# Down weights gated in every feed-forward round, sums that begin with x1, and closings on one engine

## Chip, cores and metric

The kernel runs on one core of one Trainium2 chip. The metric is the device time of one execution in microseconds (us). Before the change the median of three runs is 1894.62 us, the lowest 1893.93 and the highest 1896.67. Lower is better.

## What is computed

One encoder layer in float32 over two sequences, a prompt of 256 tokens and a sample of 1024, with a model width of 1024. A conditioning vector for each sequence gives six modulation vectors, among them the gate `g2` of the feed-forward part, so prompt and sample have different gates. The first half of the layer is attention with 16 heads and an output projection. Its result is `x` after the first layer norm, called x1 below. The second half is a gated feed-forward net of width 2816:

```python
x = _layer_norm(alpha * x + g1 * mix, ln1_g, ln1_b)          # x1

u2 = _layer_norm(x) * (1 + sc2) + sh2
f = (jax.nn.silu(u2 @ w_gate) * (u2 @ w_up)) @ w_down
return _layer_norm(alpha * x + g2 * f, ln2_g, ln2_b)          # alpha = 2 ** 0.25
```

`g2` scales the columns of `f`, which are the columns of `w_down`: `g2 * (h @ w_down)` is `h @ (w_down * g2)`.

## The kernel before

The program has five stages: modulation, projections, attention, output and the feed-forward part, which is the function `channel`. All tokens, 256 of the prompt and then 1024 of the sample, lie in ten tiles of 128. Every matrix product is made in three passes, since a float32 operand is split into a rounded high half (a copy on ScalarE) and a low half (a subtraction on VectorE): high by high, low by high and high by low (lines 218, 219 and 220). Engines run their own programs and meet by semaphores. The order of the work is written out by hand.

**Attention.** Softmax is taken with a row of negated maxima that is added to the scores through one extra row of the query tile. VectorE writes that row (line 1365), and SyncE issues a DMA that puts it in its place (line 1092) once for each of the 16 heads, g = 0 to 15. TensorE makes the scores (lines 1162 and 1163) after it has landed (`m_in`), ScalarE the exponentials (line 1295). In front of the first row SyncE's queue has the projections' stores to HBM (lines 461 and 462), and ScalarE has nothing between its last projection work and the first exponential.

**Feed-forward.** The hidden width is taken in 22 rounds f of 128 columns, and the tokens in three chunks c: tokens 0 to 256 (the prompt, tiles 0 and 1), 256 to 768 (tiles 2 to 5) and 768 to 1280 (tiles 6 to 9). A round's work:

- SyncE loads the gate and up weights of the round into `raw_gu` and the down weights into `raw_d` (lines 1832 and 1834). A load waits for the low half of the round before, the last reader of the buffer.
- ScalarE makes the high halves of `raw_gu` (line 1955) and of `raw_d` (line 1961), VectorE the low halves (lines 2058 and 2062). Each of the four has two slots, and rounds alternate between them.
- TensorE makes, for each chunk, first the down products of the *round before* for the chunk's tiles, each into one of two PSUM buffers, and then gate and up of *this* round. A down tile waits until the tile two before it was added (`dn_added`).
- ScalarE makes the silu of a chunk (line 1970) and the high half of the hidden values (line 1975), VectorE their product (line 2070) and low half (line 2076). VectorE adds each down tile to the running sum `sum_f` in SBUF (line 2122); round 0's tiles begin it with a copy (line 2119).

In a round VectorE's list for a chunk is: first add, product of the chunk before, second add, hidden low half, other adds. Behind chunk 1 stands the down weights' low half, behind chunk 2 the low half of the next round's gate and up weights.

GpSimd loads `g2`, one broadcast row for each sequence, into `gate_2` (line 1857) when the output stage is complete, and has nothing else to do until the end.

**The end.** The last round but one is added for chunks 1, 2, 0, and TensorE's list is: its down tiles of chunk 1, last gate and up of chunk 1, down tiles of chunk 2, gate and up of chunk 2, down tiles of chunk 0, then the last round's down tiles of chunk 1, gate and up of chunk 0, and the last down tiles of chunks 2 and 0. The sum of the rounds before the last is multiplied by `g2` on GpSimd (line 1862), x1 is read back from HBM (line 1844), and VectorE merges `alpha * x1` with it (line 2083). The last round alone has gated down weights (lines 2163 and 2167, the sample's in the additional buffer `down_raw_gated`). Then each tile has a last add with its row sum (line 2090), a mean and squares on ScalarE (lines 2003 and 2005), a centring with the gain on VectorE (line 2100), a root on ScalarE and a reciprocal on VectorE (line 2105). VectorE closes four of the ten tiles, 5, 8, 0 and 1, with one instruction (line 2112); the other six are scaled by ScalarE (line 2015) and closed by an add on GpSimd (line 1866). SyncE stores each tile (line 1850).

## Time and profile before

| | us |
|---|---|
| median of three runs | 1894.62 |
| the profiled execution, its own time | 1893.81 |
| span of that execution in the trace | 1892.0 |
| TensorE busy (93%) | 1754.2 |
| VectorE busy (61%) | 1146.1 |
| ScalarE busy (38%) | 710.0 |
| GpSimd busy (12%) | 224.8 |

The span goes from the first to the last instruction in the trace; the execution's own time is 1.8 us longer. Busy time is an average over stages that differ: it doesn't say which engine ends last in a stage. In the rows below, PE is TensorE, PEld its weight loads, DVE VectorE, ACT ScalarE, POOL GpSimd, and a q behind an engine's name is its queue of DMA issues. PEclk is the clock granted to TensorE as a share of full speed. In a timeline the bracket names what ended the idle time before the instruction, and how long that was.

### The profile page before, as it was taken

The page shows a single profiled execution, that of the slowest core. Times are in us where ns is not written, and L with a number is a line of the kernel's source. Part 1 is how long each engine was busy: PE and PEld are TensorE (multiplying, and loading weights), DVE is VectorE, ACT ScalarE, POOL GpSimd, SP SyncE. Part 2 cuts the span into 40 slices and gives each one's busy share as a digit, 9 for nine tenths or more (in the row PEclk, how much of TensorE's full clock was granted, in tenths as well). Part 3 has the DMA queues.
Part 4 walks back from the last instruction along what each step waited for, and adds up shares of the span by engine and source line. Part 5 has one row for each costly group of instructions (what it writes and reads, how often), then busy time and mean ns, then how long its engine had stood idle before and what let it go on. Part 6 is the DMA issues. An engine that isn't in the chain of part 4 may idle for free. (4 is left out here: it accounts for less than half of the span.)

```text
span 1892.0 us, 22484 instructions
## 1 busy us (share of the span) xinstructions
PE 1754.2 (93%) x8562; PEld 1385.6 (73%) x8562; DVE 1146.1 (61%) x1380; ACT 710.0 (38%) x1102; POOL 224.8 (12%) x237
## 2 busy tenths in 40 slices
PE   5898955999999999898999999999999999999993
PEld 3898943656667777677788888878888888878872
DVE  3888875878778776588644443444343443344388
ACT  3566543767667667654411111111111111111114
POOL 1123443101222210000000000000000000000063
PEclk8999976999999999999999999999999999999997
DMA  9133457545635541432411111111111111111123
GB/s 358 50 119 113 130 164 187 172 125 182 149 84 139 122 107 45 160 106 82 141 34 34 34 44 33 33 33 44 45 33 33 33 36 42 33 33 34 55 89 134
DMA packets 128534, 171.54 MB, mean 91 GB/s; under 512 B 15160, under 2 KB 100920, under 8 KB 125392
## 3 DMA queue, kind: packets, MB, share of 16 engines
q1 hardware_dynamic: 113184, 105.64, 18.0%
q0 software_dynamic: 12528, 46.61, 9.2%
q10 hardware_dynamic: 2752, 18.37, 3.0%
q8 instruction: 42, 0.69, 0.1%
q14 instruction: 28, 0.23, 0.0%
HBM read 128.21 MB, written 42.30 MB: 90 GB/s over the span
## 5 line engine op out<-in xcount | busy, mean ns | idle before, releaser
L2122 DVE TENSOR_TENSOR sum_f<-pair,sum_f 128x1024 f32<-128x1024 f32 x200 | 244.0, 1220 | 474.6 <-PE pair L220 473.1
L218 PE MATMUL pair<-u_hi,w_out_hi 128*128 128x512 f32 (+1 forms) x1056 | 377.2, 357 | 0.0
L220 PE MATMUL pair<-u_hi,w_out_hi 128*128 128x512 f32 (+1 forms) x1056 | 377.0, 357 | 0.0
L219 PE MATMUL pair<-u_lo,w_out_hi 128*128 128x512 f32 (+1 forms) x1056 | 376.6, 357 | 0.0
L1970 ACT ACTIVATE silu_gate<-pair 128x512 f32<-128x512 f32 (+1 forms) x63 | 33.1, 526 | 577.1 <-PE pair L220 577.1
L219 PEld LDWEIGHTS pair<-u_lo,w_out_hi 128*128 128x128 f32 x1056 | 198.6, 188 | 33.0
L218 PEld LDWEIGHTS pair<-u_hi,w_out_hi 128*128 128x128 f32 x1056 | 198.6, 188 | 32.9 <-DVE w_out_hi L1717 0.2
L220 PEld LDWEIGHTS pair<-u_hi,w_out_hi 128*128 128x128 f32 x1056 | 198.4, 188 | 32.5
L1349 DVE TENSOR_TENSOR p_lo<-p_f,p_hi 128x1024 fp32r<-128x1024 f32 (+1 forms) x144 | 167.2, 1162 | 42.8 <-ACT p_hi L1299 42.4
L218 PE MATMUL pair<-down_hi,hidden_hi 128*128 128x512 f32 x440 | 182.4, 415 | 9.7 <-DVEq L2093 6.1
L1295 ACT ACTIVATE p_f<-pair 128x1024 f32<-128x1024 f32 (+1 forms) x144 | 140.6, 976 | 132.9 <-PE pair L1163 61.9
L1357 DVE TENSOR_REDUCE max_col<-pair 128x1 f32<-128x1024 f32 x128 | 155.7, 1221 | 51.4 <-PE pair L1219 51.3
L219 PE MATMUL pair<-down_lo,hidden_hi 128*128 128x512 f32 x440 | 172.9, 393 | 0.0
L220 PE MATMUL pair<-down_hi,hidden_lo 128*128 128x512 f32 x440 | 172.6, 392 | 0.0
L1299 ACT ACTIVATE p_hi<-p_f 128x1024 fp32r<-128x1024 f32 (+1 forms) x144 | 145.8, 1012 | 4.6
L1862 POOL TENSOR_TENSOR sum_f<-sum_f,gate 128x1024 f32<-128x1024 f32 x10 | 29.9, 3010 | 880.9 <-DVE sum_f L2122 880.9
L218 PEld LDWEIGHTS pair<-down_hi,hidden_hi 128*128 128x128 f32 x440 | 82.9, 188 | 57.4 <-DVE sum_f L2122 33.4
L218 PE MATMUL pair<-p_hi,v_hi 128*65 128x512 f32 (+1 forms) x288 | 111.9, 389 | 2.0 <-DVE p_lo L1349 1.3
L219 PE MATMUL pair<-p_lo,v_hi 128*65 128x512 f32 (+1 forms) x288 | 109.9, 382 | 0.0
L220 PE MATMUL pair<-p_hi,v_lo 128*65 128x512 f32 (+1 forms) x288 | 109.8, 381 | 0.0
L1219 PE MATMUL pair<-k_a,q_a 128*128 128x512 f32 (+3 forms) x288 | 95.0, 415 | 13.2 <-DVE max_col L1357 6.5
L1975 ACT ACTIVATE hidden_hi<-hidden_f 128x512 fp32r<-128x512 f32 (+1 forms) x63 | 35.4, 561 | 168.1 <-DVE hidden_f L2070 168.1
(258 smaller groups left out, 2928.0 us busy)
## 6 DMA issues: line engine op xcount, KB each, us to landing
w_ada_late<-in_w_ada ACTq DMA_DIRECT2D x16, 1024.0 KB, 5.1
gate_up_raw<-in_w_gate SPq DMA_DIRECT2D x21, 512.0 KB, 4.0
gate_up_raw<-in_w_up SPq DMA_DIRECT2D x21, 512.0 KB, 5.2
down_raw<-in_w_down SPq DMA_DIRECT2D x21, 512.0 KB, 3.2
w_ada_first<-in_w_ada SPq DMA_DIRECT2D x8, 1024.0 KB, 13.9
o_tile<-o SPq DMA_DIRECT2D x10, 512.0 KB, 4.0
x<-y SPq DMA_DIRECT2D x10, 512.0 KB, 2.6
gate_up_raw<-x SPq DMA_DIRECT2D x10, 512.0 KB, 3.6
```

The costliest lines, as they stand in the source:

```text
L218: pe.matmul(out, a[0], b[0], start=start, stop=False)
L219: pe.matmul(out, a[0], b[1], start=False, stop=False)
L220: return pe.matmul(out, a[1], b[0], start=False, stop=stop)
L1219: mm = pe.matmul(dst, qs[0][s][0:w, q], ks[0][n][0:w, key], start=True, stop=True)
L1295: act.activation(pf[:, c % PS, 0:w], src, ACT.Exp, scale=scale).then_inc(e_done, 1)
L1299: act.activation(ph[0][:, c % PS, 0:w], pf[:, c % PS, 0:w], ACT.Copy).then_inc(p_hi, 1)
L1349: dve.tensor_tensor(ph[1][:, c % PS, 0:w], pf[:, c % PS, 0:w], ph[0][:, c % PS, 0:w], ALU.subtract).then_inc(p_lo, 1)
L1357: dve.reduce_max(mcol[:, NTP + i:NTP + i + 1], a_pair(m)[:, :, :].rearrange("p a b -> p (a b)"), AX.X).then_inc(a_free, 1)
L1862: pool.tensor_tensor(sumf[:, t, :], sumf[:, t, :], g2[:, int(t >= NTP), :], ALU.mult).then_inc(gated, 1)
L1970: act.activation(sg[:, 0:hi - lo], k.bank[(slot + c + 1) % 2][:, 0, 0:hi - lo], ACT.Silu).then_inc(silu_done, 1)
L1975: act.activation(hid[0][:, lo:hi], hf[:, 0:hi - lo], ACT.Copy).then_inc(hid_hi, 1)
L2122: dve.tensor_tensor(sumf[:, t, :], src, sumf[:, t, :], ALU.add).then_inc(dn_added, 1)
```

## The change

1. **Row 0 of the maxima** is issued by ScalarE, ahead of its first exponential. SyncE issues rows 1 to 15 as before.
2. **The gate lies in the down weights of every round.** The two slots of the down halves become two pairs of single buffers: `down_hi`, `down_lo` for the sample and `down_prompt_hi`, `down_prompt_lo` for the prompt. In each round SyncE loads the same down weights twice into `raw_d`. VectorE multiplies the first copy by the prompt's gate, the second by the sample's, and high and low halves are made of each. Per round that is one load, one copy on ScalarE and three instructions on VectorE more than before. Round 0's first product waits for `g2`.
3. **The sums begin with x1.** SyncE loads ten tiles of x1 into `sum_f` when the output stage is complete, ahead of the second down load of round 0, and the first addition is `alpha * x1 + product` in one instruction. At the end the reads of x1, the merges, GpSimd's multiplications and the buffer `down_raw_gated` fall away.
4. **VectorE closes all ten tiles.** ScalarE's scalings and GpSimd's adds fall away; GpSimd has no work left in the feed-forward part but the loads of `g2`.
5. **The last rounds.** TensorE makes the last but one round's down tiles of chunk 0 first instead of after the second gate-up chunk, so that this round is added in the order of the tiles.

The diff, without the lines that only take names away or lines that repeat:

```diff
-                k.wd = [k.sb(weights, f"down_{s}", [P, 2, D], F32R) for s in ("hi", "lo")]
+                k.wd = [k.sb(weights, f"down_{s}", [P, D], F32R) for s in ("hi", "lo")]
+                k.wdp = [k.sb(weights, f"down_prompt_{s}", [P, D], F32R) for s in ("hi", "lo")]
...
 
-        for g in range(H):
+        for g in range(1, H):
...
         k.all_read(act)
+        act.wait_ge(m_row, 1)
+        act.dma_start(qs[1][0][DA:DA + 1, :].bitcast(F32), mrow[:, :].bitcast(F32)).then_inc(m_in, 16)
...
@@ -1826,27 +1824,30 @@
...
         wg, wu, w_dn = rows(k.i["w_gate"][0]), rows(k.i["w_up"][0]), rows(k.i["w_down"][0])
 
-        def load(f):
+        def load_gate_up(f):
             sp.wait_ge(gu_lo, f)
             for m, w in enumerate((k.i["w_gate"][0], k.i["w_up"][0])):
                 sp.dma_start(raw_gu[:, m, :, :], rows(w)[:, :, bass.ds(f * P, P)]).then_inc(gu_in, 16)
-            sp.wait_ge(d_lo, f)
+
+        def load_down(f, part):
+            sp.wait_ge(d_lo, 2 * f + part)
             sp.dma_start(raw_d[:, :], k.i["w_down"][0][bass.ds(f * P, P), :]).then_inc(d_in, 16)
 
         sp.wait_ge(k.mix_ready, NT)
-        load(1)
-        with sp.Fori(2, NF) as f:
-            load(f)
-        sp.wait_ge(gu_lo, NF)
-        for i, t in enumerate(LAST_TILES):
-            if i >= 2:
-                sp.wait_ge(merged, i - 1)
-            sp.dma_start(x1[i % 2], k.x1[t * P:(t + 1) * P, :]).then_inc(x1_in[i % 2], 16)
+        load_gate_up(1)
+        after_output(sp)
+        for t in range(NT):
+            sp.dma_start(sumf[:, t, :], k.x1[t * P:(t + 1) * P, :]).then_inc(x1_in, 16)
+        load_down(0, 1)
+        load_down(1, 0)
+        with sp.Fori(2, NF - 1, 2) as f:
+            for m in range(2):
+                load_gate_up(f + m)
+                load_down(f + m - 1, 1)
+                load_down(f + m, 0)
+        load_down(LF, 1)
         for t in LAST_TILES:
-            if t in ON_DVE:
-                sp.wait_ge(dve_out, sorted(ON_DVE, key=PLACE.get).index(t) + 1)
-            else:
-                sp.wait_ge(out_ready, ON_POOL.index(t) + 1)
+            sp.wait_ge(dve_out, PLACE[t] + 1)
...
         after_output(pool)
         for s in range(2):
             pool.dma_start(g2[:, s, :], k.mod[s, 5 * D:6 * D].partition_broadcast(P)).then_inc(g2_in, 16)
-        pool.wait_ge(g2_in, 32)
-        for i, t in enumerate(LAST_TILES):
...
-            pool.wait_ge(dn_added, NT * (LF - 1) + i + 1)
-            pool.tensor_tensor(sumf[:, t, :], sumf[:, t, :], g2[:, int(t >= NTP), :], ALU.mult).then_inc(gated, 1)
...
@@ -1872,9 +1863,11 @@
             place = t if place is None else place
...
+            hi, lo = wdp if t < NTP else wd
             for m in range(2):
+                cols = slice(m * 512, (m + 1) * 512)
                 mm = three(pe, k.bank[2 + t % 2][:, m, :], [x[:, t * P:(t + 1) * P] for x in hid],
-                           [w[:, 1 - slot, m * 512:(m + 1) * 512] for w in wd], True, True)
+                           [hi[:, cols], lo[:, cols]], True, True)
...
                     pe.wait_ge(hid_lo, NCH * (f - 1) + c + 1)
                     if c == 0:
-                        pe.wait_ge(d_lo, f)
+                        pe.wait_ge(d_lo, 2 * f - 1)
+                    if c == 1:
+                        pe.wait_ge(d_lo, 2 * f)
                     for t in TILES[c]:
...
         def before_last_down(c):
 
...
-            pe.wait_ge(d_lo, LF)
+            pe.wait_ge(d_lo, 2 * LF - (c == 0))
             for t in TILES[c]:
-                down(LF, t, 1, PLACE[t])
+                down(LF, t, 1)
 
...
+            pe.wait_ge(d_lo, 2 * NF - (c == 0))
             for t in TILES[c]:
-                down(NF, t, 1 if c == 0 else 0, PLACE[t])
+                down(NF, t, 0, PLACE[t])
 
         def finale():
+            before_last_down(0)
             before_last_down(1)
             last_gate_up(0)
             before_last_down(2)
             last_gate_up(1)
-            before_last_down(0)
             last_down(0)
...
-        def d_round(f, slot, first):
-            act.wait_ge(d_in, 16 * (f + 1))
+        def prompt_round(f, first):
+            act.wait_ge(d_gated, 2 * f + 1)
             if not first:
-                act.wait_ge(dn_ready, NT * (f - 1))
-            act.activation(wd[0][:, slot, :], raw_d[:, :], ACT.Copy).then_inc(d_hi, 1)
+                act.wait_ge(dn_ready, NT * (f - 1) + NTP)
+            act.activation(wdp[0][:, :], raw_d[:, :], ACT.Copy).then_inc(d_hi, 1)
+
+        def sample_round(f, first):
+            act.wait_ge(d_gated, 2 * f + 2)
+            if not first:
+                act.wait_ge(dn_ready, NT * f)
+            act.activation(wd[0][:, :], raw_d[:, :], ACT.Copy).then_inc(d_hi, 1)
...
                 if not (first and c == 0):
                     silu(f, c, slot)
                 if c == 1:
-                    d_round(f, slot, isinstance(f, int) and f < 2)
+                    prompt_round(f, isinstance(f, int) and f == 0)
                 if c == 2:
                     gu_round(f + 1, 1 - slot, isinstance(f, int) and f == 0)
+                    sample_round(f, isinstance(f, int) and f == 0)
...
         def finale():
             silu(LF, 0, 1)
-            act.wait_ge(wd_gated, 1)
-            act.wait_ge(dn_ready, NT * (LF - 1))
-            act.activation(wd[0][:, 1, :], raw_s[:, :], ACT.Copy).then_inc(d_hi, 1)
+            prompt_round(LF, False)
             last_silu(0)
+            sample_round(LF, False)
             last_silu(1)
             for m, g in enumerate(("ln2_g", "ln2_b")):
...
             dve.wait_ge(gu_hi, f + 1)
             dve.tensor_tensor(wgu[1][:, slot, :, :, :], raw_gu[:, :, :, :], wgu[0][:, slot, :, :, :], ALU.subtract).then_inc(gu_lo, 1)
 
-        def d_low(f, slot):
-            dve.wait_ge(d_hi, f + 1)
-            dve.tensor_tensor(wd[1][:, slot, :], raw_d[:, :], wd[0][:, slot, :], ALU.subtract).then_inc(d_lo, 1)
+        def gate_prompt(f):
+            dve.wait_ge(d_in, 32 * f + 16)
+            dve.tensor_tensor(raw_d[:, :], raw_d[:, :], g2[:, 0, :], ALU.mult).then_inc(d_gated, 1)
...
+        def prompt_low(f):
+            dve.wait_ge(d_hi, 2 * f + 1)
+            dve.tensor_tensor(wdp[1][:, :], raw_d[:, :], wdp[0][:, :], ALU.subtract).then_inc(d_lo, 1)
...
 
             i = PLACE[t]
             dve.wait_ge(dn_ready, NT * LF + i + 1)
-            dve.wait_ge(merged, i + 1)
+            dve.wait_ge(dn_added, NT * (LF - 1) + t + 1)
             dve.scalar_tensor_tensor(z[:, t, :], k.bank[2 + t % 2][:, :, :].rearrange("p a b -> p (a b)"), 1.0, sumf[:, t, :],
...
             if isinstance(f, int) and f == 1:
-                dve.tensor_copy(sumf[:, t, :], src).then_inc(dn_added, 1)
+                if t == 0:
+                    dve.wait_ge(x1_in, 16 * NT)
+                dve.scalar_tensor_tensor(sumf[:, t, :], sumf[:, t, :], ALPHA, src, ALU.mult, ALU.add).then_inc(dn_added, 1)
...
                         hidden_low(f, c)
+                if c == 0 and not first:
+                    gate_prompt(f)
                 if c == 1:
-                    d_low(f, slot)
+                    if first:
+                        dve.wait_ge(g2_in, 32)
+                        gate_prompt(f)
+                    prompt_low(f)
                 if c == 2:
+                    gate_sample(f)
                     gu_low(f + 1, 1 - slot)
+                    sample_low(f)
...
         def finale():
-            add(LF, 2, 0)
+            add(LF, 0)
             product(LF, 0, 1)
-            add(LF, 3, 1)
+            add(LF, 1)
             hidden_low(LF, 0)
-            dve.wait_ge(g2_in, 32)
-            dve.wait_ge(d_in, 16 * NF)
-            dve.tensor_tensor(raw_s[:, :], raw_d[:, :], g2[:, 1, :], ALU.mult).then_inc(wd_gated, 1)
-            add(LF, 4, 2)
-            add(LF, 5, 3)
-            dve.wait_ge(wd_gated, 1)
-            dve.tensor_tensor(raw_d[:, :], raw_d[:, :], g2[:, 0, :], ALU.mult).then_inc(wd_gated, 1)
-            dve.wait_ge(d_hi, NF)
-            dve.tensor_tensor(wd[1][:, 1, :], raw_s[:, :], wd[0][:, 1, :], ALU.subtract).then_inc(d_lo, 1)
-            merge(2)
-            merge(3)
+            gate_prompt(LF)
+            for t in TILES[1]:
+                add(LF, t)
+            prompt_low(LF)
             last_product(0)
-            add(LF, 6, 4)
             last_low(0)
-            add(LF, 7, 5)
-            merge(4)
-            add(LF, 8, 6)
...
+            for t in TILES[2]:
+                add(LF, t)
+            sample_low(LF)
             last_product(1)
-            add(LF, 0, 8)
             last_low(1)
-            add(LF, 1, 9)
-            dve.wait_ge(d_hi, NF + 1)
-            dve.tensor_tensor(wd[1][:, 0, :], raw_d[:, :], wd[0][:, 0, :], ALU.subtract).then_inc(d_lo, 1)
             for t in (2, 3, 4, 5):
                 last_add(t)
```

VectorE's order where round 0 passes into round 1, before the change (`pair` is a PSUM buffer, `w_out_hi` the memory of the gate-up halves, the shapes are those of the output):

```order
L2070 TENSOR_TENSOR hidden_f32<-pair0,silu_gate 128x256
L2076 TENSOR_TENSOR hidden_lo<-hidden_f32,hidden_hi 128x256
L2062 TENSOR_TENSOR down_lo<-down_raw,down_hi 128x1024
L2070 TENSOR_TENSOR hidden_f32<-pair1,silu_gate 128x512
L2076 TENSOR_TENSOR hidden_lo<-hidden_f32,hidden_hi 128x512
L2058 TENSOR_TENSOR w_out_hi<-gate_up_raw,w_out_hi 128x2x8x128
L2119 COPY sum_f<-pair2 128x1024
```

and after it:

```order
L2069 TENSOR_TENSOR hidden_f32<-pair0,silu_gate 128x256
L2075 TENSOR_TENSOR hidden_lo<-hidden_f32,hidden_hi 128x256
L2049 TENSOR_TENSOR down_raw<-down_raw,gate_2 128x1024
L2057 TENSOR_TENSOR down_prompt_lo<-down_raw,down_prompt_hi 128x1024
L2069 TENSOR_TENSOR hidden_f32<-pair1,silu_gate 128x512
L2075 TENSOR_TENSOR hidden_lo<-hidden_f32,hidden_hi 128x512
L2053 TENSOR_TENSOR down_raw<-down_raw,gate_2 128x1024
L2045 TENSOR_TENSOR w_out_hi<-gate_up_raw,w_out_hi 128x2x8x128
L2061 TENSOR_TENSOR down_lo<-down_raw,down_hi 128x1024
L2113 SCALAR_TENSOR_TENSOR sum_f<-sum_f,pair2 128x1024
```

Two products with `gate_2` stand there now, the second in front of the low half of round 1's gate and up weights, and the sum's first instruction is a multiply-add on itself instead of a copy.

SyncE's issues at the start of the feed-forward part, before (the branch opens the loop of the rounds):

```order
L1825 UNCONDITIONAL_BRANCH
L1832 DMA gate_up_raw<-in_w_gate 128x8x128
L1832 DMA gate_up_raw<-in_w_up 128x8x128
L1834 DMA down_raw<-in_w_down 128x1024
L1838 UNCONDITIONAL_BRANCH
L1832 ISA
L1832 DMA gate_up_raw<-in_w_gate 128x8x128
```

and after:

```order
L1823 UNCONDITIONAL_BRANCH
L1830 DMA gate_up_raw<-in_w_gate 128x8x128
L1830 DMA gate_up_raw<-in_w_up 128x8x128
L1840 DMA sum_f<-x1 128x1024 x10
L1834 DMA down_raw<-in_w_down 128x1024 x2
L1843 UNCONDITIONAL_BRANCH
L1830 ISA
```

Ten loads of x1 stand between the gate-up weights of round 1 and the down loads, of which there are two in a row: round 0's second and round 1's first.

VectorE's last rows before (L2100 centres, L2105 inverts, L2112 closes):

```order
L2105 RECIPROCAL std_e<-std_e 128x1
L2100 SCALAR_TENSOR_TENSOR sum_f<-final_rows,neg_mean 128x1024
L2105 RECIPROCAL std_e<-std_e 128x1
L2100 SCALAR_TENSOR_TENSOR sum_f<-final_rows,neg_mean 128x1024
L2105 RECIPROCAL std_e<-std_e 128x1
L2112 SCALAR_TENSOR_TENSOR final_rows<-sum_f,std_e,final_rows 128x1024
L2100 SCALAR_TENSOR_TENSOR sum_f<-final_rows,neg_mean 128x1024 x2
L2105 RECIPROCAL std_e<-std_e 128x2
L2112 SCALAR_TENSOR_TENSOR final_rows<-sum_f,std_e,final_rows 128x1024 x2
```

and after, where the same are L2092, L2097 and L2104:

```order
L2104 SCALAR_TENSOR_TENSOR final_rows<-sum_f,std_e,final_rows 128x1024
L2097 RECIPROCAL std_e<-std_e 128x1
L2092 SCALAR_TENSOR_TENSOR sum_f<-final_rows,neg_mean 128x1024
L2104 SCALAR_TENSOR_TENSOR final_rows<-sum_f,std_e,final_rows 128x1024
L2097 RECIPROCAL std_e<-std_e 128x1
L2092 SCALAR_TENSOR_TENSOR sum_f<-final_rows,neg_mean 128x1024
L2104 SCALAR_TENSOR_TENSOR final_rows<-sum_f,std_e,final_rows 128x1024
L2092 SCALAR_TENSOR_TENSOR sum_f<-final_rows,neg_mean 128x1024
L2097 RECIPROCAL std_e<-std_e 128x2
L2104 SCALAR_TENSOR_TENSOR final_rows<-sum_f,std_e,final_rows 128x1024 x2
```

A closing now stands between nearly every two centrings.

## Rows read from the trace of the kernel before

**Rows 1.** Stretches by engine: from, length, busy us and instructions each, PEclk, DMA, GB/s.

```profile
944.00:1799.00 855.00, 852.79 (x4083) 691.36 (x4082) 364.79 (x360) 120.37 (x160) 0.00 (x0) 1.00 0.13 37
1799.00:1892.00 93.00, 59.39 (x264) 46.02 (x262) 82.67 (x72) 29.80 (x53) 47.03 (x16) 0.85 0.32 113
```

**Rows 2.** Timeline before the first scores: start, length, engine, line; releaser in brackets.

```profile
304.01 0.28 DVE L1365 TENSOR_SCALAR neg_max_row<-pair 10x128 fp32r<-10x128 f32 x1 [0.47 <-PE pair L1225]
...
307.40 1.65 SPq L461 DMA_DIRECT2D kn_t_lo_rows<-x_hat  x1
309.10 0.89 SPq L1092 DMA_DIRECT2D q_b<-neg_max_row  x1
312.28 1.16 POOL L1120 MEMSET k_b<- 1x1280 f32 x1 [19.81 <-DMA kn_t_lo_rows<-x_hat]
...
312.33 0.55 PE L1162 MATMUL pair<-q_a,k_a 128*128 128x256 f32 x1 [6.71 <-issue]
...
313.63 1.28 ACT L1295 ACT_TABLE_LOAD   x1 [24.35 <-PE pair L1163]
```

**Rows 3.** DMA issues of the whole span: KB each, median us to landing.

```profile
down_raw<-in_w_down SPq DMA_DIRECT2D x21, 512.0 KB, 3.2
...
gate<-mod_rows POOLq DMA_DIRECT2D x2, 512.0 KB, 4.3
...
va_hi_rows<-va_hi SPq DMA_DIRECT2D x10, 64.0 KB, 1.5
...
v_hi<-va_hi_rows POOLq DMA_DIRECT2D x2, 320.0 KB, 11.9
```

**Rows 4.** Stretches by engine: the first loads.

```profile
5.00:10.00 5.00, 0.00 (x0) 0.00 (x0) 2.98 (x6) 1.58 (x3) 0.00 (x0) 1.00 1.03 419
```

**Rows 5.** Timeline of round 0 and the first down tiles.

```profile
931.66 1.11 POOL L1857 DMA_DIRECT2D gate<-mod_rows  x2 [157.90 <-DVE u_lo L1725]
...
932.70 1.04 ACT L1961 ACTIVATE down_hi<-down_raw 128x1024 fp32r<-128x1024 f32 x1
...
933.77 1.23 DVE L2062 TENSOR_TENSOR down_lo<-down_raw,down_hi 128x1024 fp32r<-128x1024 f32 x1 [0.52 <-ACT down_hi L1961]
...
938.11 2.29 DVE L2058 TENSOR_TENSOR w_out_hi<-gate_up_raw,w_out_hi 128x2048 fp32r<-128x2048 f32 x1 [1.12 <-ACT w_out_hi L1955]
...
944.25 0.40 PE L218 MATMUL pair<-down_hi,hidden_hi 128*128 128x512 f32 x1
...
947.01 0.28 PE L218 MATMUL pair<-u_hi,w_out_hi 128*128 128x256 f32 x1
```

**Rows 6.** Stretches by engine: around TensorE's pause at the end of the output stage.

```profile
921.40:924.90 3.50, 0.37 (x2) 0.00 (x0) 3.40 (x6) 0.29 (x1) 0.00 (x0) 1.00 0.37 150
924.90:930.00 5.10, 5.03 (x19) 4.14 (x20) 0.01 (x1) 3.87 (x9) 0.00 (x0) 0.67 0.76 206
```

**Rows 7.** Groups of instructions: VectorE's adds, 944 to 1799.

```profile
L2122 DVE TENSOR_TENSOR sum_f<-pair,sum_f 128x1024 f32<-128x1024 f32 x190 | 231.9, 1221 | 465.3 <-PE pair L220 463.9
```

**Rows 8.** Timeline of the end: TensorE's first matmuls, VectorE's closing run.

```profile
1798.81 0.40 PE L218 MATMUL pair<-down_hi,hidden_hi 128*128 128x512 f32 x1
...
1804.90 0.39 PE L218 MATMUL pair<-u_hi,w_out_hi 128*128 128x512 f32 x1
...
1816.09 0.39 PE L218 MATMUL pair<-down_hi,hidden_hi 128*128 128x512 f32 x1
...
1851.67 0.42 DVE L2148 TENSOR_TENSOR hidden_f<-pair,silu_gate 128x256 f32<-128x256 f32 x1 [2.31 <-ACT silu_gate L1994]
...
1852.01 1.27 DVE L2100 SCALAR_TENSOR_TENSOR sum_f<-final_rows,neg_mean 128x1024 f32<-128x1024 f32 x1
...
1886.35 2.48 DVE L2112 SCALAR_TENSOR_TENSOR final_rows<-sum_f,std_e,final_rows 128x1024 f32<-128x1024 f32 x2
```

**Rows 9.** Groups of instructions: VectorE, 1799 to 1892.

```profile
L2112 DVE SCALAR_TENSOR_TENSOR final_rows<-sum_f,std_e,final_rows 128x1024 f32<-128x1024 f32 x4 | 9.0, 2276 | 0.1
...
L2105 DVE RECIPROCAL std_e<-std_e 128x1 f32<-128x1 f32 x4 | 0.6, 150 | 0.0
```

67 lines of the change are left out of this document (22 added, 45 removed).

## Prediction

> **What bounds the kernel now.** I read the stretches first. In the feed-forward rounds TensorE is busy 852.8 of 855.0 us at full clock, VectorE only 364.8 [rows 1]. There the bound is TensorE, and other engines' work is free as long as no wait reaches it. The last 93 us differ: TensorE 59.4, VectorE 82.7, GpSimd 47.0 [rows 1], and the program ends with VectorE's last two closing instructions [rows 8]. Then I looked for the holes in TensorE's row next to the three places that the change touches. Before the first attention scores it stands for 6.71 us, released by nothing the profile names, 3 us after SyncE issues row 0 [rows 2]. At the start of round 1 it has no hole: round 1's gate-up begins at 947.01 [rows 5], and its weights' low half, begun at 938.11 and 2.29 long, was ready at 940.4. That slack of 6.6 us is what the change spends.
>
> **Row 0.** VectorE has the row at 304.29, but SyncE's queue still has stores to issue, the last of them at 307.40, and issues the row at 309.10; TensorE starts at 312.33 [rows 2]. ScalarE has idled 24.35 us by then [rows 2] and now issues it at about 304.35. How long it travels the trace doesn't show for this queue: 1.5 us is the median of SyncE's 64 KB stores [rows 3], 3.2 us what the row took on SyncE's queue behind stores (309.10 to 312.33). So it lands between 305.8 and 307.6. I take 307.0, nearer the upper end since the engines are full of stores: TensorE starts 5.3 us earlier (4.7 to 6.5). What follows is TensorE, ScalarE and VectorE waiting on each other, with no time fixed from outside before the feed-forward, so the gain is kept.
>
> The Trainium skill (DMA: Bandwidth & Descriptors, section Issuing engines are not separate DMA queues) speaks against such a move: all issuing engines share the same 16 DMA engines, and another issuer saves only the time to start a transfer. By that rule the saving would be 309.10 less 304.35, 4.8 us, as that time is large here.
>
> **Round 0.** Three transfers now gate it. (a) Ten rows of x1 go out on SyncE's queue once u2 is complete, at about 931.4; the two gate rows go out on GpSimd's at 931.66 [rows 5]. That is 12 times 0.52 MB, 6.3 MB; long bursts moved at 419 GB/s [rows 4], so 15.0 us. (b) VectorE's prompt product waits for the gate rows. They took 4.3 us alone [rows 3]; sharing the engines evenly with x1 they need about 2.1 MB of traffic, 5 us, from 933: 938.2. Then the product, the high copy and the low half, 1.23 (priced as the low half of the same two-operand form), 1.04 and 1.23 [rows 5], give 941.9. The first down tiles, at 944.25 [rows 5], don't notice. (c) Only then is the second down load issued, behind x1 on the same queue: 931.4, 1 us to start, 15.0, its own 1.25, and half a microsecond to land, 949.2. VectorE sits on it with the low half of round 1's gate-up weights queued behind: product and low half, 1.2 and 2.3, end at 952.8. TensorE needs that at 947.0, so it stops for **5.8 us**. ScalarE's copy of the gate-up high half is in front of its own wait and is not late.
>
> After a hole of 3.5 us the next 5.1 us ran at a mean clock of 0.67 [rows 6], which is 3.4 us at half speed, 1.7 us lost. For a hole of 5.8 I put 2.1. Round 0 costs **7.9 us**. The low bound is a load that needs only its usual 3.2 us [rows 3] from 941.9: 945.1, TensorE at 948.7, cost 1.7. The high bound is the first rival.
>
> **Rounds 1 to 20.** Each gets two products and one more low half on VectorE (3 times 1.22, from the 1.23 of rows 5), one more copy on ScalarE (1.04) and one more load. VectorE idles 465.3 us before the adds [rows 7], 23.3 per round, so 3.7 fit. Position counts more than the sum. The prompt product stands behind the second add of a round, while TensorE runs the 256-column chunk of about 5.6 us. The sample product, the gate-up low half and the sample low half follow the last add, 4.7 us within a chunk of 11.2 us [rows 8]. The order of adds, hidden products and hidden low halves, which sets the short stalls of today, is unchanged. The loads have over 8 us each from issue to use, against 3.2 [rows 3]. So nothing. Without that cover it would be up to 3.7 us times 20. The first adds become multiply-adds of the same operand sizes: nothing.
>
> **The end.** Counted from round 20's first down tile, 1798.81, the span ends 93.2 us later [rows 8]. A tile costs 1.38 (947.01 less 944.25, halved, [rows 5]), a 512-column chunk 11.2 (1804.90 to 1816.09 [rows 8]). Now ten tiles and two chunks precede the last ones: 13.8 and 22.4. Stalls: the fifth tile waits for the third's add, behind two adds, product, hidden low half and gate product: 1.9 in all. After the first chunk the third tile waits for an add behind silu, product, copy, low half and gate product: 5.2 against two tiles' 2.75, so 2.5. Sum 40.6. Then four tiles (5.5), one stall of 1.5 for the first closing add, the 256-column chunk (5.6) and silu: the last hidden product starts at 53.7, where before it was 52.9 (1851.67).
>
> From there VectorE runs without a gap: product and low half 0.42 each, ten centrings at 1.27, six last adds at 1.3 (an add of 1.22 [rows 7] and its accumulator), ten closings at 1.24 (half of the last 2.48), seven small reciprocals at 0.15 [rows 9], less 0.08 of overlap at each of some 35 starts (the first product ends 0.08 after the next start at 1852.01 [rows 8]): 33.0 us. Before, the same run took 37.2 (1851.67 to 1888.83 [rows 8]), with four closings of mean 2276 ns beside GpSimd [rows 9]; GpSimd is silent now, so 1.24 stands. With the 3.2 us of the last store: 53.7, 33.0 and 3.2 make 89.9, a gain of 3.3; I take **3.0**, as a hole of 2.5 us can cost some clock. Bounds: 0 (two such losses of 1.7) and 5.0 (no stalls of the first kind).
>
> **The sum.** 5.3 and 3.0 off, 7.9 on: minus 0.4 against the profiled execution's 1893.81 (span 1892.0, 1.8 around it), 1893.4. The median of the three runs lies 0.8 above that execution, so I put the time at 1894.0, no measurable difference. Bound by bound (row 0 4.7 to 6.5; round 0 from 5.8 without clock loss to 10.7 with a tenth less bandwidth and twice the loss; end 0 to 5) the independent errors give about 4 us either way.
>
> **Rivals.**
> 1. *Slower: the gate rows wait behind x1.* GpSimd's loads of 320 KB took 11.9 us next to a full SyncE queue [rows 3], and if the gate rows come last, at 948, the prompt weights are ready at 951.5, so even the first down tiles stop; the second load is issued only then: 954.7, and gate-up starts at 958.3. Cost 11.3 and 2 of clock, 13.3 in all. Time 1893.8 less 5.3 and 3.0, plus 13.3: 1898.8. It decides from a gate arrival after 942.3, and makes the whole slower by over 0.2% from about 947. For it: that row, and ten transfers on one queue against two on the other. Against: the gate rows are issued as early as x1's first [rows 5], while those loads came when SyncE's queue already had several of its own in flight. Chance 0.12.
>
> The Trainium skill (same page, section Queues, rings and completion order) says that each DMA engine takes turns between its queues; by that the gate rows come at 938 and this rival has no price. The 11.9 us [rows 3] speak against turns that are that even.
> 2. *Row 0 isn't faster,* as the stores keep the DMA engines until the same time. Gain 0 to 0.5: 1898.5. For it: the store issued last before the row released GpSimd only at 312.28 [rows 2]. Against: the row is ten rows of 128 words, 5 KB, and has a queue to itself. Chance 0.08.
> 3. *Faster: the second load doesn't queue behind x1.* Round 0 then costs 1.7 and the sum is minus 6.6: 1887.2 to 1888. For it: SyncE's issue alone is free by 937. Against: one queue; row 0 itself came only after the stores ahead of it [rows 2]. Chance 0.12.
> 4. *The rounds stall after all,* as the down weights have one buffer each where there were two halves: half a microsecond per round is plus 10, 1904. Against: TensorE reads them 19 us after their last reader ends in the tightest place. Chance 0.04.
>
> The forecast has 0.64. It is within 0.2% (3.8 us, about what a measurement here can tell from no change) in most of its spread; 0.08 of it falls below, 0.04 above. With the rivals: faster 0.20, same 0.62 (0.52 of the forecast, the rest from rivals 1 and 2 near the bound), slower 0.18. The range takes the forecast's 4 us and reaches to rivals 1 and 2 on one side and 3 on the other: 1888 to 1899.5.
>
> **What would show it.** Row 0: the first scores near 307 instead of 312.3. Round 0: VectorE idle before the sample product until about 949 less the 5.3 of shift, and a TensorE hole of some 6 us before round 1's gate-up with half clock behind it. Rounds: still 42.7 us each from down tile to down tile. End: about 90 us from round 20's first tile, closings at 1.24 and GpSimd empty. The forecast is wrong if the hole in round 0 is under 3 or over 10 us, if the rounds grow, or if the closing run isn't near 33 us.

## The result, and the profile after

The changed kernel takes 1902.23 us (median of six, 1900.8 to 1904.92), the kernel before 1894.94 beside it: a ratio of 1.004 with an interval of 1.003 to 1.005. It is slower by 7.3 us, where 1894 and no difference were forecast, and the time lies above the range of 1888 to 1899.5. The profiled execution has a span of 1900.2 us against 1892.0, 8.2 us more. Where they arise is read by laying TensorE's row of both traces side by side: how much later or earlier does the same matmul start?

| stretch | forecast | measured |
|---|---|---|
| to the last matmuls of the output stage (row 0) | -5.3 | -1.7 |
| round 0, to the second tile chunk of round 1 | +7.9 | +10.7 |
| rounds 1 to 19 | 0 | +0.2 |
| from round 20's first down tile to the end | -3.0 | -1.1 |
| sum (rounded) | -0.4 | +8.2 |

The first timeline, which answers [rows 2]: row 0 now goes out on ScalarE's queue, 0.4 us after VectorE began it, but VectorE has it 2.9 us later than before. ScalarE's load of its function table (ACT_TABLE_LOAD), which stood behind the first scores before (313.63 [rows 2]), now lies in the wait for the row. So the first exponential starts 2.0 us earlier (312.95 against 314.92), the first scores only 0.6.

```profile
306.92 0.28 DVE L1368 TENSOR_SCALAR neg_max_row<-pair 10x128 fp32r<-10x128 f32 x1 [0.47 <-PE pair L1226]
307.31 0.85 ACTq L1330 DMA_DIRECT2D q_b<-neg_max_row  x1
...
308.19 1.28 ACT L1296 ACT_TABLE_LOAD   x1 [19.45 <-DVE neg_max_row L1368]
...
311.73 0.55 PE L1163 MATMUL pair<-q_a,k_a 128*128 128x256 f32 x1 [3.19 <-issue]
```

Round 0 in the timeline, which answers [rows 5]:

```profile
930.20 5.15 SPq L1840 DMA_DIRECT2D sum_f<-x  x10
...
930.49 1.11 POOL L1858 DMA_DIRECT2D gate<-mod_rows  x2 [158.46 <-DVE u_lo L1728]
...
940.02 1.23 DVE L2049 TENSOR_TENSOR down_raw<-down_raw,gate 128x1024 f32<-128x1024 f32 x1 [7.94 <-DMA gate<-mod_rows]
...
943.63 12.25 SPq L1834 DMA_DIRECT2D down_raw<-in_w_down  x2
943.75 0.47 PE L219 MATMUL pair<-down_prompt_hi,hidden_hi 128*128 128x512 f32 x1 [1.02 <-DVE down_prompt_lo L2057]
...
950.96 1.23 DVE L2053 TENSOR_TENSOR down_raw<-down_raw,gate 128x1024 f32<-128x1024 f32 x1 [5.36 <-DMA down_raw<-in_w_down]
952.10 2.28 DVE L2045 TENSOR_TENSOR w_out_hi<-gate_up_raw,w_out_hi 128x2048 fp32r<-128x2048 f32 x1
```

The chain is the one that was forecast: g2, the prompt's product, the second down load, the sample's product, the low half behind it. One more link showed: TensorE stands 1.0 us before its first down tile too. The same stretch by engine shows TensorE's hole and the clock behind it:

```profile
943.50:946.60 3.10, 2.85 (x12) 2.17 (x12) 1.40 (x3) 2.37 (x2) 0.00 (x0) 1.00 1.02 414
946.60:954.40 7.80, 0.13 (x1) 0.00 (x0) 3.44 (x3) 1.62 (x3) 0.00 (x0) 0.78 0.29 114
954.40:962.00 7.60, 7.56 (x50) 7.52 (x51) 5.78 (x6) 0.73 (x2) 0.00 (x0) 0.78 0.69 201
```

The list of waits names both sides:

```profile
PE pair L219 <- DVE w_out_hi L2045: 7.7, 1, 7.7
DVE down_raw L2049 <- DMA gate<-mod_rows: 7.9, 1, 7.9
...
DVE down_raw L2053 <- DMA down_raw<-in_w_down: 5.4, 1, 5.4
```

The rounds and the end by stretch, which answers [rows 1]. VectorE works 70 us more in the rounds and TensorE does not notice; in the end GpSimd is silent and VectorE has 25 us less to do:

```profile
954.00:1808.00 854.00, 851.34 (x4068) 690.37 (x4069) 434.55 (x422) 141.31 (x179) 0.00 (x0) 1.00 0.16 50
1808.00:1900.20 92.20, 60.83 (x266) 47.57 (x264) 57.70 (x68) 23.62 (x47) 0.00 (x0) 0.85 0.20 74
```

The last stretches hold a hole that before had no counterpart: TensorE stands 2.3 us before the third of four down tiles, which starts at 1834.85, and then runs at 0.63 of the clock on the mean.

```profile
1829.60:1834.70 5.10, 2.92 (x13) 2.06 (x11) 3.56 (x4) 1.24 (x2) 0.00 (x0) 1.00 0.00 0
1834.70:1839.30 4.60, 4.45 (x13) 3.54 (x14) 2.45 (x3) 0.00 (x0) 0.00 (x0) 0.63 0.00 0
```

The closing run (groups of VectorE, which answer [rows 8, 9]) is as forecast: ten closings at 1.28 us, none beside GpSimd, and 33.3 us from the last hidden product (1863.77) to the last closing's end (1894.57 and 2.48).

```profile
L2104 DVE SCALAR_TENSOR_TENSOR final_rows<-sum_f,std_e,final_rows 128x1024 f32<-128x1024 f32 x10 | 12.6, 1280 | 0.4 <-ACT final_rows L2007 0.3
```

### The profile page after: what moved, and what is told of

Its sections match the earlier page's. It is cut to its first block and busy times, and to the rows that moved or that the text cites. A ratio compares the mean times of both kernels' runs of the same rounds, so it can differ in the third digit from the quotient of the medians.

```text
span 1900.2 us, 22724 instructions
## 1 busy us (share of the span) xinstructions
PE 1757.3 (92%) x8562; PEld 1388.1 (73%) x8562; DVE 1191.9 (63%) x1439; ACT 726.7 (38%) x1117; POOL 178.4 (9%) x221
## 5 line engine op out<-in xcount | busy, mean ns | idle before, releaser
L1971 ACT ACTIVATE silu_gate<-pair 128x512 f32<-128x512 f32 (+1 forms) x63 | 33.3, 528 | 492.2 <-PE pair L221 492.2
L219 PE MATMUL pair<-down_hi,hidden_hi 128*128 128x512 f32 x352 | 147.9, 420 | 9.2 <-DVE sum_f L2116 3.5
L220 PE MATMUL pair<-down_lo,hidden_hi 128*128 128x512 f32 x352 | 139.5, 396 | 0.0
L221 PE MATMUL pair<-down_hi,hidden_lo 128*128 128x512 f32 x352 | 139.0, 395 | 0.0
L219 PEld LDWEIGHTS pair<-down_hi,hidden_hi 128*128 128x128 f32 x352 | 66.6, 189 | 51.8 <-DVE sum_f L2116 34.7
L219 PE MATMUL pair<-w_in_hi,u_hi 128*128 128x384 f32 (+1 forms) x240 | 85.6, 357 | 1.2 <-DVE u_lo L881 1.2
```

What stands on the lines that cost most here:

```text
L219: pe.matmul(out, a[0], b[0], start=start, stop=False)
L220: pe.matmul(out, a[0], b[1], start=False, stop=False)
L221: return pe.matmul(out, a[1], b[0], start=False, stop=stop)
L1971: act.activation(sg[:, 0:hi - lo], k.bank[(slot + c + 1) % 2][:, 0, 0:hi - lo], ACT.Silu).then_inc(silu_done, 1)
```

## Experiments

Twelve kernels ran, in three groups, each group on one chip with the kernel before beside it (medians 1894.17, 1895.42 and 1895.24). The changed kernel stands 7.3 us above the kernel before in the result and 5.6 in the third group (`after_again`), with intervals that overlap; a gain counted from it by medians has that spread. The profiles tell more: laid beside the profile of before, matmul against matmul as in the table of the result, they differ by (us)

| kernel | up to round 0's last gate and up | from there into round 1 | from round 20's first down tile on |
|---|---|---|---|
| after | -1.7 | +10.7 | -1.1 |
| after_again | -2.3 | +10.9 | -1.1 |
| e1_no_x1 | -2.8 | +0.8 | -1.1 |
| e5_x1_scalar | -3.3 | +10.5 | -1.1 |
| e4_low_first | +0.6 | +6.1 | -2.7 |
| e6_round0 | -3.0 | +8.8 | -1.2 |
| e9_three | -0.5 | +2.2 | -2.7 |
| e7a_order | -3.7 | +11.8 | -5.8 |
| e7_tail | -2.2 | +10.9 | -9.3 |
| e2_row0_sync | +1.8 | +10.9 | -1.1 |
| e3_row0_alone | -0.5 | 0.0 | 0.0 |
| e10_all | -3.6 | +2.0 | -8.6 |
| e11_hidden_first | -1.5 | +1.7 | -8.6 |

The middle column is what round 0 costs, the last what the end costs. The rounds between differ by 0.3 us or less. In the last column `e4_low_first` and `e9_three`, whose end is unchanged, stand apart by the clock alone (see the last section).

### Is x1 the cause of round 0's hole?

`e1_no_x1` takes the ten loads away, and with them `alpha * x1` out of the result:

```diff
-        after_output(sp)
-        for t in range(NT):
-            sp.dma_start(sumf[:, t, :], k.x1[t * P:(t + 1) * P, :]).then_inc(x1_in, 16)
...
-                dve.scalar_tensor_tensor(sumf[:, t, :], sumf[:, t, :], ALPHA, src, ALU.mult, ALU.add).then_inc(dn_added, 1)
+                dve.tensor_copy(sumf[:, t, :], src).then_inc(dn_added, 1)
```

> The changed kernel without the ten loads of x1 at the start; the first add is a copy again, so the residual term alpha*x1 is left out of the result and only the time is of use. Theory (x1 in front of the second down load in SyncE's queue, and beside g2 on the same DMA engines, makes round 0's hole): g2 lands near 936 instead of 940, the second down load near 943.5 instead of 950.9, round 1's gate and up weights are ready near 946.7, and TensorE's hole there falls from 7.9 to under 1 us with no half clock behind it. Round 0's cost of 10.7 goes almost whole: 1892 us (1891 to 1893.5). Rival (the gate products and the single raw buffer make the chain too long even without x1): a hole of 4 us or more stays, 1898 or slower.

It took 1890.96 us, a ratio of 0.9982 (0.9973 to 0.9991) to the kernel before: 3.2 us below it, where the changed kernel stands 5.6 to 7.3 above. In its profile round 0 costs 0.8 us instead of 10.7. In the timeline the second load is waited for 1.4 us instead of 5.4, and TensorE's hole is 0.5 us:

```profile
938.07 8.26 SPq L1834 DMA_DIRECT2D down_raw<-in_w_down  x2
...
941.40 1.23 DVE L2050 TENSOR_TENSOR down_raw<-down_raw,gate 128x1024 f32<-128x1024 f32 x1 [1.37 <-DMA down_raw<-in_w_down]
...
944.88 0.38 PE L219 MATMUL pair<-u_hi,w_out_hi 128*128 128x256 f32 x1 [0.48 <-DVE w_out_hi L2042]
```

The theory stands: without x1 beside them the gate products, the second load and the single buffers cost 0.8 us in its profile.

### The queue, or the bytes?

`e5_x1_scalar` issues the same ten loads from ScalarE:

```diff
                 if c == 1:
+                    if first:
+                        for t in range(NT):
+                            act.dma_start(sumf[:, t, :], k.x1[t * P:(t + 1) * P, :]).then_inc(x1_in, 16)
                     prompt_round(f, isinstance(f, int) and f == 0)
```

> The changed kernel with the ten loads of x1 on ScalarE's queue, issued in round 0 between the first hidden high half and the prompt's copy, so the second down load has SyncE's queue to itself; the bytes are the same. Theory (the load waits for its turn behind x1 in one queue): with x1 on another queue the two take turns, the 0.52 MB take some 2.5 us at half of 419 GB/s and 1 to 2 us around it, landing at 947 to 948 instead of 950.9; the hole shrinks from 7.9 to 4 to 5 us and the kernel is 3 to 4 us faster than the changed kernel, which stands 7.3 above the kernel before: 3.5 to 4.5 above it. Rival (what counts is the sum of the bytes on the 16 DMA engines, not the queue): landing still near 950, hole near 7, no gain over 1 us.

It took 1901.87 us, a ratio of 1.0036 (1.0022 to 1.0049): no gain that can be told from none, a hole of 8.0 us and 10.5 us for round 0. My theory of one queue fell. The load alone on SyncE's queue, issued at 940.17, was used at 948.42, 8.2 us later, against 7.3 in the changed kernel. Two views of the DMA packets show why, the first of 940.2 to 943.9, the second of 944 to 946 (queue, packets, MB, share of the engines' time; q1 is SyncE's queue, q10 ScalarE's):

```profile
q10 hardware_dynamic: 418, 1.52, 102.2%
q1 hardware_dynamic: 4, 0.02, 1.1%
```

```profile
q10 hardware_dynamic: 114, 0.40, 50.4%
q1 hardware_dynamic: 99, 0.41, 50.4%
```

For 3.7 us after its issue the load moved 4 packets, 0.02 of its 0.52 MB, while all queues together moved 416 GB/s; only then did the two share evenly. So a queue of its own brought the load its share, but late.

The Trainium skill (DMA: Bandwidth & Descriptors, section Issuing engines are not separate DMA queues) says that DMAs of every issuer run on the same 16 engines and interleave; no gain from another issuer agrees with it. The same page (section Queues, rings and completion order) lets each engine take turns between its queues; the equal halves from 944 on agree, the 3.7 us before them are not in that rule.

### VectorE's place in the line

`e4_low_first` leaves the loads alone and moves one instruction in round 0:

```diff
                 if c == 2:
-                    gate_sample(f)
                     gu_low(f + 1, 1 - slot)
+                    gate_sample(f)
                     sample_low(f)
```

> The changed kernel with VectorE's low half of round 1's gate and up weights in front of the sample's gate product, in round 0 alone. The second down load stays behind x1. Theory (the hole of 7.9 us is VectorE sitting on that load with the low half queued behind it): the low half starts when its high half is done, 946.7, and ends at 949.0; the hole is 2.5 us, half clock costs up to 1.7 behind it, and of round 0's cost of 10.7 some 5 stay: 1896.5 (1895 to 1898). Rival (the stall only moves to the sample's down tiles, which need the late load too): a hole of 3 us or more before the first sample tile of round 1, gain under 2.5, 1900 or slower.

It took 1896.37 us, a ratio of 1.0012 (1.0003 to 1.0021): 2.2 above before, within the range that was expected. In its profile round 0 costs 6.1 us instead of 10.7. The hole is 2.3 us long, and what ends it is ScalarE's high half, made late because ScalarE too had waited for g2. A second hole of 1.2 us, before the third down tile of round 1, is the small part in which the rival was right.

```profile
948.44 2.29 DVE L2045 TENSOR_TENSOR w_out_hi<-gate_up_raw,w_out_hi 128x2048 fp32r<-128x2048 f32 x1 [1.11 <-ACT w_out_hi L1950]
...
950.78 0.58 PE L219 MATMUL pair<-u_hi,w_out_hi 128*128 128x256 f32 x1 [2.32 <-DVE w_out_hi L2045]
```

### x1 in parts

`e6_round0` adds to `e4_low_first` that eight of the ten tiles go behind the second down load:

```diff
-        for t in range(NT):
+        for t in range(NTP):
             sp.dma_start(sumf[:, t, :], k.x1[t * P:(t + 1) * P, :]).then_inc(x1_in, 16)
         load_down(0, 1)
+        for t in range(NTP, NT):
+            sp.dma_start(sumf[:, t, :], k.x1[t * P:(t + 1) * P, :]).then_inc(x1_late, 16)
         load_down(1, 0)
```

> The changed kernel with round 0 put in another order: SyncE loads two tiles of x1, then the second down weights, then the other eight tiles of x1 (with a semaphore of their own, for which the add of tile 2 waits); and VectorE makes the low half of round 1's gate and up weights before the sample's gate product, in round 0 alone. Theory: g2 lands near 937, the second down load near 944, no hole over 1 us is left in TensorE's row there and no half clock; of round 0's cost of 10.7 at most 1 stays: 9.7 to 10.5 us faster than the changed kernel, 2 to 3 below the kernel before. Rival (eight late tiles of x1 hold up the add of tile 2 and the first down load of round 1): a new hole of 2 us or more near the chunk of tokens 256 to 768 of round 1, gain 5 to 8.

It took 1899.42 us, a ratio of 1.0019 (1.001 to 1.0028), 4 above the kernel before; in its profile round 0 costs 8.8 us. The forecast was wrong and the rival half right. A hole came up in round 1, of 5.1 us, through one of the rival's two causes: not the wait for the tiles of x1, but round 1's own first down load. The gain is smaller than the rival's 5 to 8 us. Issued at 948.51 behind the eight tiles, it is used at 956.37, and the add of tile 2, for which TensorE waits, stands behind that product on VectorE:

```profile
948.51 0.33 SPq L1834 DMA_DIRECT2D down_raw<-in_w_down  x1
...
956.37 1.23 DVE L2051 TENSOR_TENSOR down_raw<-down_raw,gate 128x1024 f32<-128x1024 f32 x1 [4.42 <-DMA down_raw<-in_w_down]
957.51 1.22 DVE L2117 SCALAR_TENSOR_TENSOR sum_f<-sum_f,pair 128x1024 f32<-128x1024 f32 x1
```

`e9_three` puts four tiles ahead of that load and four behind:

```diff
-        for t in range(NTP, NT):
+        for t in TILES[1]:
+            sp.dma_start(sumf[:, t, :], k.x1[t * P:(t + 1) * P, :]).then_inc(x1_mid, 16)
+        load_down(1, 0)
+        for t in TILES[2]:
             sp.dma_start(sumf[:, t, :], k.x1[t * P:(t + 1) * P, :]).then_inc(x1_late, 16)
-        load_down(1, 0)
```

> e6_round0 with x1 in three parts on SyncE's queue: tiles 0 and 1, round 0's second down weights, tiles 2 to 5, round 1's first down weights, tiles 6 to 9; each part has its own semaphore. Theory (e6's hole of 5.2 us came from VectorE waiting for round 1's first down load behind eight tiles of x1, with the add of tile 2 queued behind that wait): that load lands near 952, when VectorE comes to it, the hole of 5.2 us and its half clock go, about 6.5 us less than e6_round0, and the kernel stands 2 to 3 us below the kernel before. Rival (the whole traffic of x1 only finds another victim, the gate and up loads of round 2 or the add of tile 6): a new hole of 2 us or more later in round 1, at or above the kernel before.

It took 1891.78 us, a ratio of 0.9983 (0.9974 to 0.9992): 3.5 below the kernel before. `after_again`, the changed kernel in the same group, took 1900.86 (ratio 1.0032, 1.002 to 1.0045), 9.1 us more. In the profiles that order gives back 8.5 us of round 0's 10.7. The longest hole left there is 1.1 us.

### The end

`e7a_order` changes VectorE's order in the last rounds, `e7_tail` in addition fills its idle time before the last hidden product:

```diff
             hidden_low(LF, 0)
-            gate_prompt(LF)
             for t in TILES[1]:
                 add(LF, t)
+            gate_prompt(LF)
             prompt_low(LF)
             last_product(0)
+            add(LF, 6)
             last_low(0)
-            gate_sample(LF)
-            for t in TILES[2]:
+            for t in (7, 8, 9):
                 add(LF, t)
+            gate_sample(LF)
             sample_low(LF)
...
+            for t in (2, 3, 4):
+                centre(t)
             last_product(2)
-            centre(2)
+            centre(5)
             last_low(2)
-            centre(3)
...
-            centre(4)
-            centre(5)
```

> The changed kernel with another order on VectorE in the last rounds alone: the prompt's gate product behind the four adds of chunk 1, and in chunk 2 the first add ahead of the hidden low half and the sample's gate product behind the adds. Theory (the holes of 1.4 us before the fifth down tile of round 20 and of 2.5 us before its ninth come from VectorE's order, and the second one sets off 1.7 us of half clock): all three go, the last hidden product starts 5.6 us earlier after round 20's first tile, 50.1 instead of 55.7; 4.5 to 5.6 us faster than the changed kernel, 2 to 3 above the kernel before. Rival (half clock there doesn't come from the hole, or the holes only move): gain of 2 us or less.

> The order of e7a_order, and three of the four first centrings put in front of the last hidden product, where VectorE idles 4.8 us. Theory (the closing run is VectorE's own 33.3 us from that product on, so what moves in front of it comes off the end): 3.6 us faster than e7a_order. Rival (the centrings wait for means that ScalarE makes late and hold up the product, or stores or ScalarE's squares become the end): gain of 1.5 us or less.

They took 1897.2 us (1.0011, 1.0002 to 1.002) and 1893.86 us (0.9993, 0.9984 to 1.0002). Against the changed kernel, 5.6 to 7.3 above the kernel before, the order is worth 3.8 to 5.5 us, and the filling 3.3 more. In the profiles the end is 4.7 us shorter by the order and 3.5 more by the filling, both as expected. The two stretches of `e7a_order` that answer the ones with the hole above have none, and the clock stays whole:

```profile
1827.50:1835.00 7.50, 7.42 (x31) 5.47 (x30) 6.08 (x7) 1.23 (x2) 0.00 (x0) 1.00 0.00 0
1835.00:1844.80 9.80, 9.80 (x43) 7.87 (x42) 2.38 (x3) 1.06 (x1) 0.00 (x0) 1.00 0.00 0
```

In `e7_tail` the three centrings stand in VectorE's row before the last hidden product at 1858.62:

```profile
1853.97 3.68 DVE L2092 SCALAR_TENSOR_TENSOR sum_f<-final_rows,neg_mean 128x1024 f32<-128x1024 f32 x3
```

### Row 0

`e2_row0_sync` undoes the move in the changed kernel, `e3_row0_alone` makes it alone in the kernel before:

```diff
-        for g in range(H):
+        for g in range(1, H):
...
         k.all_read(act)
+        act.wait_ge(m_row, 1)
+        act.dma_start(qs[1][0][DA:DA + 1, :].bitcast(F32), mrow[:, :].bitcast(F32)).then_inc(m_in, 16)
```

> The changed kernel with row 0 issued by SyncE again. Theory (the move saves what the trace shows from row to first scores, 4.8 against 8.3 us, and the maxima came 2.9 us later in the profile of the changed kernel for a reason that has nothing to do with the move): 3.5 us slower than the changed kernel, 1905.7, and the maxima at the same times as with the move. Rival (the net 1.7 us that the first scores came earlier is all, the later maxima being part of the move's price): 1903.9.

> The kernel before with nothing changed but row 0 issued by ScalarE. Theory: 3.5 us faster than before, 1891.4. Rival (net gain only 1.7): 1893.2. If the row's travel were unchanged, 1894.9.

> The changed kernel itself, on the same chip as the others of this call: 7 to 8 us above the kernel before. Its profile tells whether the maxima before the first scores, which came 2.9 us later than in the profile of before, differ from execution to execution: 304 to 307 us, with the scores 4.6 to 5.6 us behind.

`e2_row0_sync` took 1903.29 us, 9.1 above the kernel before (ratio 1.0049, 1.0035 to 1.0062) where the changed kernel stands 5.6 to 7.3 above it. That would make the move worth 1.8 to 3.5 us, but the intervals overlap. `e3_row0_alone` took 1893.18, 1.0 less than before (0.9989, 0.998 to 0.9998); its runs spread from 1889.56 to 1894.99. Both times lie at or nearer the rivals' figures, so my 3.5 was too much. `after_again`, 5.6 above the kernel before, came out under the 7 to 8 that were expected. The reason is in the fourteen profiles. Of each, the start of the instruction that makes the row and of the first scores:

| kernel | issued by | row, us | first scores, us | difference |
|---|---|---|---|---|
| before | SyncE | 304.01 | 312.33 | 8.3 |
| e2_row0_sync | SyncE | 305.79 | 313.15 | 7.4 |
| after | ScalarE | 306.92 | 311.73 | 4.8 |
| after_again | ScalarE | 305.18 | 310.28 | 5.1 |
| e3_row0_alone | ScalarE | 305.87 | 310.45 | 4.6 |
| the other nine | ScalarE | 303.99 to 307.15 | 308.62 to 311.94 | 4.6 to 6.5 |

The row itself comes anywhere between 304.0 and 307.2, whoever issues it. A later row is not the price of the move, which the rival took it for: the keys that the maxima need land at different times, and the first product of the maxima, which waits for them, starts 11.3 to 11.5 us before the row in every profile. In the two profiles with SyncE the stores in front of it hold the scores until 312.3 and 313.2, though the rows differ by 1.8; with ScalarE they follow the row, 310.3 on the mean of twelve. Against 312.7, the mean of the two with SyncE, that is 2.4 us; 3.4 us in the six profiles with a row before 304.5 (scores at 309.3) and 0.9 in the three with a row after 306.8 (311.8).

The first exponential gains more, 3.8 us on the mean (311.5 against 315.3): in all twelve profiles with ScalarE its table load of 1.28 us lies in the wait for the row, in the two with SyncE behind the scores. Just before the first down tiles 2.9 us are left, again against two profiles alone.

Where the row spends its time on ScalarE's queue, the packets tell. In the changed kernel it is issued at 307.31. The first view is from 307.4 to 310, the second from 310 to 311.2 (the row is q10, SyncE's stores q1):

```profile
q1 hardware_dynamic: 1449, 0.90, 110.0%
```

```profile
q1 hardware_dynamic: 772, 0.38, 110.1%
q10 hardware_dynamic: 20, 0.01, 1.9%
```

While the stores moved 346 GB/s, none of the row's packets went out for 2.7 us. In the twelve profiles its first packet starts 2.6 to 3.9 us after the issue.

### All together

`e10_all` is `e9_three` with the end of `e7_tail`; `e11_hidden_first` moves, in round 0 alone, the work that waits for g2 behind the hidden values of chunk 1:

```diff
                 if c == 1:
-                    prompt_round(f, isinstance(f, int) and f == 0)
+                    if not first:
+                        prompt_round(f, False)
                 if c == 2:
                     gu_round(f + 1, 1 - slot, isinstance(f, int) and f == 0)
+                    if first:
+                        prompt_round(f, True)
...
-                if c == 1:
-                    if first:
-                        dve.wait_ge(g2_in, 32)
-                        gate_prompt(f)
+                if c == 1 and not first:
                     prompt_low(f)
                 if c == 2 and first:
+                    dve.wait_ge(g2_in, 32)
+                    gate_prompt(f)
+                    prompt_low(f)
                     gu_low(f + 1, 1 - slot)
```

> e9_three with the last rounds of e7_tail. If both theories hold the gains add up: about 10 us from round 0 and 8.8 from the end, 18 to 19 us faster than the changed kernel, 11 to 12 below the kernel before, a ratio near 0.994 to it. If round 0's rival holds, a ratio of 0.997 or more.

> e10_all with one more change of order in round 0: ScalarE makes the hidden values of chunk 1 and round 1's gate and up high half before the prompt's high half, and VectorE the hidden product and its low half before the prompt's gate product, so that neither waits for g2 first. Theory (the 1.1 us that were left before round 1's gate and up in e6_round0 come from that wait): 1 us faster than e10_all. Rival (the prompt's low half now comes later than the first down tile wants it): no gain, or up to 1 us slower.

They took 1885.56 us (0.9954, 0.994 to 0.9967) and 1885.35 us (0.9945, 0.9931 to 0.9958). Both beat the kernel before, by about 10 us, and the changed kernel of the same group by 15.3 and 15.5; 18 to 19 had been expected of the first. That sum was too high: in the profiles round 0's part is 8.5 us and the end's 8.2, 16.7 together, and `e10_all` has 16.3 of them in the same two stretches. The interval of the ratio leaves 2.5 us either way, so that it isn't shown that a part got lost. `e11_hidden_first` was to be 1 us faster still and gains nothing that can be told from none: the hole of 0.6 us before round 1's gate and up is gone in its profile, but the one before the third down tile grew from 1.0 to 1.4.

## Why the prediction was wrong

**Row 0: the size of the term.** SyncE's stores in front of the row were the right thing to leave. But I priced the travel on ScalarE's queue at 2.7 us, between the median of SyncE's 64 KB stores (1.5) and 3.2 [rows 2, 3]; it is 4.2 to 6.1 from issue to scores, since the row's packets start 2.6 to 3.9 us after the issue beside those stores. And I took 304.29 for the row from one execution, which showed it early: the fourteen profiles reach to 307.2. The bound of 4.7 was built on the same two numbers, so it could not hold them. The gain was 1.7 us and not 5.3, which makes 3.6 of the 8.6 us by which the sum of the profile was off. Even so there was luck in the 1.7: the scores came only 0.6 us earlier, and the table load, which the prediction does not mention, brought the exponentials 1.4 more. The rival for row 0, a gain of 0 to 0.5, was too low as well.

**Round 0: the right chain, 2.8 us too short.** Times here are put back by the 1.7 us that TensorE was early, so that they compare with the forecast's. I expected g2 at 938.2 and first down tiles that don't notice; g2 came at 941.7 and the tiles were 1.2 us late. The gate rows' first packet started 3.2 us after the issue, where it takes 1.3 without x1 beside it (`before`, `e1_no_x1`, `e3_row0_alone`), and then they took 6.0 us instead of 5. 941.7 stayed under the 942.3 from which the first rival decided, and that rival, g2 behind all of x1, was not it. I expected the second load at 949.2; it was used at 952.6. Thirteen transfers of 0.52 MB moved at 386 GB/s and not at the 419 of [rows 4], which is 1.4 us on 6.8 MB, and from the last full microsecond to the use 2 us passed where I had put a half. So the hole was 7.9 us (954.44 less 943.75, less the 2.76 of two tiles) against 5.8. The half clock cost 1.6 us against 2.1. That the high bound of 10.7 is what came is luck: it was written for worse bandwidth and twice the clock loss, and late tiles and a late landing filled it.

```profile
931.20:948.00 16.80, 14.51 (x62) 11.14 (x60) 4.17 (x5) 4.41 (x5) 0.40 (x1) 1.00 0.98 386
948.00:949.00 1.00, 0.00 (x0) 0.00 (x0) 0.00 (x0) 0.00 (x0) 0.00 (x0) 1.00 0.78 299
949.00:951.00 2.00, 0.00 (x0) 0.00 (x0) 0.04 (x1) 0.00 (x0) 0.00 (x0) 0.99 0.04 8
```

Against the third rival, a second load that doesn't queue behind x1, the prediction set "one queue". The load did wait, but `e5_x1_scalar` shows that another queue would not have helped.

**Rounds 1 to 20: right.** Nothing was forecast and 0.2 us came. The adds' idle time fell from 465.3 us [rows 7] to 400.7, which is 3.2 us a round out of 23.3; so the products did stay out of TensorE's way:

```profile
L2116 DVE TENSOR_TENSOR sum_f<-pair,sum_f 128x1024 f32<-128x1024 f32 x190 | 232.0, 1221 | 400.7 <-PE pair L221 399.2
```

**The end: the clock's term.** The closing run was 33.3 us for 33.0, but the forecast's own terms for it add up to 32.0, so that it came so near by a slip in the sum. The stalls of 1.9, 2.5 and 1.5 came as worked out (2.0, 2.5 and 1.4 from start to start). The last hidden product stands 55.7 us behind round 20's first tile and not 53.7, since half clock behind the second of them cost 1.7 us, for which 0.3 had been left. `e7a_order` takes hole and half clock away together.

All three errors lay on one side, and the range had been made as if they were independent. Two have one source, transfers priced by rows in which they had less beside them: in both, the first packet started some 3 us after the issue.

## What to carry to other kernels

Moving a load out of the end of a kernel into its middle is not free just because the middle is bound by another engine: ten tiles of 0.52 MB at once are 12.5 us of all DMA engines at 419 GB/s [rows 4], and the next load that someone needs came late behind them, on SyncE's queue and, with x1 on ScalarE's, on another. Issue such a load in the pieces and in the order in which they are wanted, between the loads with a date (`e9_three`, 8.5 us of round 0), and put instructions that wait for a transfer behind those that another engine waits for (`e4_low_first`, 4.6 us). The same holds for products that are wanted later than the adds behind them (`e7a_order`, 4.7 us of the end). A time read in one execution has a spread: compare it with other rows of its kind before it becomes a term, above all where it ends in a DMA.
